# A modulation vector formed by GpSimd beside the delta rule

## The reference

```python
mod = jax.nn.silu(c) @ w_ada[layer] + b_ada[layer]      # (1, 1024) @ (1024, 3072)
shift, scale, gate = jnp.split(mod[:, None, :], 3, axis=-1)
h = rms_norm(x, norm_g[layer]) * (1.0 + scale) + shift
```

## Time and profile before

| | us |
|---|---|
| median of three runs | 3007.29 |
| lowest, highest | 3001.44, 3011.1 |
| the profiled execution | 3002.61 |
| its span | 3000.8 |
| mean granted clock of TensorE | 0.963 of full |
| TensorE busy | 2821.8 |
| VectorE busy | 1661.6 |
| GpSimd busy | 928.9 |
| ACT busy | 676.1 |

### The profile page before, as it was taken

How to read it: one execution, slowest core, us unless ns; L and a number is a source line. 1 busy time by engine, 2 the same in 40 slices (tenths; PEclk the granted TensorE clock), 3 DMA queues, 4 the chain that set the end, 5 groups by cost and what they waited for, 6 DMA issues and landing times.

```text
span 3000.8 us, 34181 instructions
## 1 busy us (share of the span) xinstructions
PE 2821.8 (94%) x14231; PEld 2381.3 (79%) x14231; DVE 1661.6 (55%) x2160; ACT 676.1 (23%) x1063; POOL 928.9 (31%) x510
## 2 busy tenths in 40 slices
PE   6999999989998999999999998999999999978798
PEld 5787799877777788878888877788888888867577
DVE  4789755664512555454444478522465556466556
ACT  3112222233322420000000032211222222234342
POOL 1422000016631613332332235653111221211454
PEclk9999888889999999999999999999999999989899
DMA  3223223225311421111111134552322333354573
GB/s 136 65 92 116 77 82 99 74 68 191 125 56 64 155 92 50 49 57 42 43 56 43 42 108 159 203 169 92 127 92 99 99 118 121 117 191 172 197 263 133
DMA packets 134270, 325.10 MB, mean 108 GB/s; under 512 B 11724, under 2 KB 49508, under 8 KB 133988
## 3 DMA queue, kind: packets, MB, share of 16 engines
q1 hardware_dynamic: 61632, 165.70, 17.3%
q10 hardware_dynamic: 72484, 157.22, 14.6%
HBM read 245.26 MB, written 77.61 MB: 108 GB/s over the span
## 4 chain that ended last, share of the span: by engine, by line
PE 77%; DVE 12%; ACT 3%; DMA 3%; issue 2%; POOL 1%; ACTq 1%; DVEq 0%; POOLq 0%
PE pp L286 25%; PE pp L268 21%; PE pp L471 7%; PE pp L1931 5%; PE pp L2506 4%; DMA ret_m<-m_s 2%; PE pp L1176 2%; PE pp L1406 1%; PE pp L1837 1%; DVE ffn_cb L2111 1%; POOL w_lo L3088 1%; PE pp L1429 1%; DVE hgin_b L2321 1%; PE pp L1817 1%; PE pp L1433 1%
## 5 line engine op out<-in xcount | busy, mean ns | idle before, releaser
L3086 POOL CAST w_hi<-w_raw 128x1024 fp32r<-128x1024 f32 x252 | 292.9, 1162 | 1976.9 <-PE pp L286 844.8
L3088 POOL TENSOR_TENSOR w_lo<-w_raw,w_hi 128x1024 fp32r<-128x1024 f32 x252 | 640.5, 2542 | 20.2
L286 PE MATMUL pp<-w_hi,act_hi 128*128 128x512 f32 x1344 | 548.8, 408 | 25.7 <-POOL w_lo L3088 10.5
L286 PE MATMUL pp<-w_hi,act_lo 128*128 128x512 f32 x1344 | 532.8, 396 | 0.0
L286 PE MATMUL pp<-w_lo,act_hi 128*128 128x512 f32 x1344 | 531.4, 395 | 0.0
L286 PEld LDWEIGHTS pp<-w_hi,act_hi 128*128 128x128 f32 x1344 | 257.6, 192 | 84.8 <-POOL w_lo L3088 15.3
L286 PEld LDWEIGHTS pp<-w_hi,act_lo 128*128 128x128 f32 x1344 | 256.8, 191 | 59.4
L286 PEld LDWEIGHTS pp<-w_lo,act_hi 128*128 128x128 f32 x1344 | 257.7, 192 | 51.6
L268 PE MATMUL pp<-act_lo,w_hi 128*128 128x512 f32 (+1 forms) x944 | 290.7, 389 | 0.0
L268 PE MATMUL pp<-act_hi,w_hi 128*128 128x512 f32 (+1 forms) x944 | 290.7, 389 | 0.0
L268 PE MATMUL pp<-act_hi,w_lo 128*128 128x512 f32 (+1 forms) x944 | 290.6, 389 | 0.0
(11 more groups left out here) (393 smaller groups left out, 4131.7 us busy)
## 6 DMA issues: line engine op xcount, KB each, us to landing
w_raw<-in_weights SPq DMA_DIRECT2D x292, 512.0 KB, 3.5
z_s<-hg_st ACTq DMA_DIRECT2D x52, 512.0 KB, 3.0
hg_qkb<-hT_s SPq DMA_DIRECT2D x18, 512.0 KB, 7.1
qkvT_s<-mixin_o ACTq DMA_DIRECT2D x12, 512.0 KB, 2.8
gdn_qkv<-qkvT_s ACTq DMA_DIRECT2D x8, 768.0 KB, 5.0
front_x<-in_x ACTq DMA_DIRECT2D x8, 512.0 KB, 5.7
mix_x<-in_x ACTq DMA_DIRECT2D x8, 512.0 KB, 5.5
x_s<-mix_y ACTq DMA_DIRECT2D x8, 512.0 KB, 2.9
```

The source lines that it names most:

```text
L286: last = pe.matmul(dst, a[:, k, t * P:(t + 1) * P], columns(w, j, k, 0, n), start=(k == 0 and a is high and w is w_hi), stop=(k == NK - 1 ...
L3086: pool.tensor_copy(hi, raw).then_inc(w_split, 1)
L3088: pool.tensor_tensor(lo, raw, hi.bitcast(F32), ALU.subtract).then_inc(w_ready, 1)
```

## The change

GpSimd gets a new routine, `sum_ada`, which it runs after `move_mem`. For each of the twelve strips and each half it multiplies the half (four k by 256 columns) by `ada_c`, repeated over the columns, in one 128x1024 instruction, counts the half as let go, adds four blocks to two (128x512), and two to one (128x256); for the second half it adds the two halves too. That is seven dependent instructions, each waited for through `ada_summed`. The sums and the products lie in the space of `w_hi`, free in these rounds. TensorE then adds over partitions only: two matmuls a strip, with the sum stationary and a column of ones moving. It waits for the strip's seven steps instead of the loads, and counts `ada_turned`, for which VectorE waits instead of `w_ready`. GpSimd splits the first output weights only when all twelve are kept.

```diff
+            def sum_ada(self, pool):
+                after(pool, self.src.an, f"gate{self.src.GATES - 1}", 0)
+                tt, n = pool.tensor_tensor, 0
+
+                def step(ins):
+                    nonlocal n
+                    n += 1
+                    ins.then_inc(self.ada_summed, 1)
+                    pool.wait_ge(self.ada_summed, n)
+
+                m = self.ada_parts
+                for j, out in enumerate(self.ada_sum):
+                    strip = FIRST_STRIP[f"ada{j}"]
+                    for half in range(2):
+                        pool.wait_ge(w_loaded[half], (RAW_AT[strip] // 2 + 1) * 16)
+                        pool.wait_ge(w_ready, halves_ready(strip, half))
+                        w = w_raw[:, half * HALF:(half + 1) * HALF].rearrange("p (k n) -> p k n", n=SC)
+                        c = ada_c[:, half * NK // 2:(half + 1) * NK // 2].rearrange("p (k a) -> p k a", a=1).broadcast_to((P, NK // 2, SC))
+                        step(tt(m[:, :, :], w, c, ALU.mult))
+                        pool.sem_inc(w_ready, 1)
+                        step(tt(m[:, 0:2, :], m[:, 0:2, :], m[:, 2:4, :], ALU.add))
+                        if half == 0:
+                            step(tt(out[:, :], m[:, 0, :], m[:, 1, :], ALU.add))
+                        else:
+                            step(tt(m[:, 0, :], m[:, 0, :], m[:, 1, :], ALU.add))
+                            step(tt(out[:, :], out[:, :], m[:, 0, :], ALU.add))
+                assert n == self.ADA_STEPS * N_ADA
+
+            ADA_STEPS = 7
...
                 def ada(j):
-                    strip = FIRST_STRIP[f"ada{j}"]
                     if j:
                         pe.wait_ge(self.ada_kept, j)
                     if prep:
                         after(pe, self.pv, "l3", p)
-                    for half in range(2):
-                        pe.wait_ge(w_loaded[half], (RAW_AT[strip] // 2 + 1) * 16)
+                    pe.wait_ge(self.ada_summed, (j + 1) * self.ADA_STEPS)
                     for m in range(2):
-                        for k in range(NK):
-                            c = k * SC + m * P
-                            last = pe.matmul(bank(self.K_)[:, m:m + 1], w_raw[:, c:c + P], ada_c[:, k:k + 1], start=(k == 0), stop=(k == NK - 1))
-                            if m == 1 and k == NK // 2 - 1:
-                                last.then_inc(w_ready, 1)
-                    last.then_inc(w_ready, 1)
+                        last = pe.matmul(bank(self.K_)[:, m:m + 1], self.ada_sum[j][:, m * P:(m + 1) * P], ones[:, 0:1], start=True, stop=True)
+                    last.then_inc(self.ada_turned, 1)
...
                 def ada(j):
-                    dve.wait_ge(w_ready, halves_ready(FIRST_STRIP[f"ada{j}"], 2))
+                    dve.wait_ge(self.ada_turned, j + 1)
...
                     delta.move_mem(pool)
+                    delta.sum_ada(pool)
+                    pool.wait_ge(delta.ada_kept, N_ADA)
                     pool.wait_ge(w_ready, halves_ready(j, 0))
```

More of the change, by code:

```diff
@@ L172, in build @@
         w_raw = place("w_raw", [P, STRIP])
+        w_hi_at = top["at"]
         w_hi = [place(f"w_hi{s}", [P, HALF], F32R) for s in range(4)]
@@ L1050, in __init__ @@
                 self.mem_moved, self.mem_kept = sem("gdn_mem_moved"), sem("gdn_mem_kept")
+                ada_sums = {"at": w_hi_at}
+                self.ada_sum = [place(f"gdn_ada_sum{j}", [P, SC], F32, ada_sums) for j in range(N_ADA)]
+                self.ada_parts = place("gdn_ada_parts", [P, NK // 2, SC], F32, ada_sums)
+                assert ada_sums["at"] <= w_hi_at + 4 * 4 * HALF
+                self.ada_summed = sem("gdn_ada_summed")
                 self.ada_stored, self.ada_turned = sem("gdn_ada_stored"), sem("gdn_ada_turned")
@@ L1363, in act @@
                     if o == NT - 1:
-                        act.wait_ge(self.ada_turned, 1)
+                        act.wait_ge(self.ada_turned, N_ADA + 1)
                         act.activation(self.mr[:, :], bank(self.F_)[0:3 * NK, 0:P], ACT.Copy).then_inc(self.ada_turned, 1)
-                        act.wait_ge(self.ada_turned, 2)
+                        act.wait_ge(self.ada_turned, N_ADA + 2)
                         act.dma_start(mod_s.rearrange("o (c p) -> (o c) p", p=P), self.mr[:, :]).then_inc(self.ada_stored, 16)
```

## The result

The changed kernel takes 3022.7 us in the median of four runs (3019.4 to 3024.2), the kernel before 3006.3 (now four runs): ratio 1.0059, 95% interval 1.0043 to 1.0074. It is slower, by 18 us if one goes by the ratio (16 between the medians); 38 were forecast. The profiled execution's span is 3022.4 us. L1639 and L1642 are now the steps that take a level's result (L1609, L1612); take care not to read the new L1639 as the old mask.

The account below looks back on a forecast made before the run. TensorE was taken to bound the rounds. Rounds 4 to 7 (+17 us), 1 to 3 (+20) and 0 (+2.5), less 1 or 2 for existing waits, gave +38 on 3007.3: 3045 us, range 3020 to 3078.

Parts of the forecast that it names:

- TensorE's work: In the ada product, L1406: 48.7 us of matmuls go, 6 us of one-column products come, 43 us gained if nothing else happened.
- No slack before a first strip: Before a round's first strip: round 1's loads land at 401.6 us and L1406 starts at 401.95, so no slack.
- GpSimd's price: GpSimd's seven steps: multiply 2.34 us, adds 1.2 and 0.65, with pauses 9.6 us a strip, 115 in twelve.
- Rival C: GpSimd's multiply with a repeated input costs 4.7 us, making the kernel dearer: 3074 to 3103 us; chance 0.12.
- First strip: Before L1418 in round 1: the sum comes 4.2 us later with strict turns, 2.7 without; rounds 4 to 7 cost 17 us.
- the turns: In the rounds, GpSimd and some VectorE SBUF steps stop each other for whole instructions; some twenty VectorE steps a round affected.
- Second strips: In rounds 1 to 3, GpSimd's second strip delays VectorE's mask and level 5's result: +7 us a round, +20 in all.
- The sum: Over the eight rounds: 17 + 20 + 2.5 = 39.5 us, less 1 or 2 for existing waits, so +38 us.
- rival A: Only the latency of first strips costs, VectorE's idle time swallowing the turns: +21 us, 3028 us; chance 0.20.
- Rival B: TensorE's clock in the rounds rises over 0.9, since one-column products lower it and waiting does not: 2980 us; chance 0.06.
- three signs of being wrong: In the rounds: VectorE steps keep their times, sums are ready before TensorE asks, or the granted clock rises to 0.95.

Follow-up runs that it names:

- e13: Changed kernel with GpSimd's seven steps replaced by 57 tiny 128x1 memsets a strip, the wait kept: 1.0064 of the kernel before.
- e1: Kernel before, TensorE's 16 products a strip kept, plus GpSimd's seven steps on other data, awaited only by ACT at the rounds' end: 1.0071 of the kernel before.
- e2: Kernel before with only two one-column products a strip, straight from w_raw, and GpSimd idle: 0.9855 of the kernel before.
- e7: e5 with GpSimd's seven steps replaced by tiny memsets, 50 a strip: 2935.5 us, 0.9778 of the kernel before.
- e5: Changed kernel with TensorE's two products a strip moved to the middle of the next round, same GpSimd work: 2991.6 us, 0.9966 of the kernel before.
- e3: Changed kernel with GpSimd's seven steps replaced by long memsets of about the same lengths that read nothing: 1.0023 of the kernel before.
- e14: e1 with chains of tiny 128x1 memsets in place of GpSimd's seven steps: 1.0003 of the kernel before.

## Why the prediction was wrong

The direction, the place and the wait were right; the size was not, 38 us against 18. Its steps in order:

- *TensorE's work.* 48.7 us go and 48 short records come: right (page: 40 us less busy over the program).
- *No slack before a first strip.* Right: the load lands, GpSimd starts 0.1 us later, TensorE stands 5.68 us where it had worked 3.8.
- *GpSimd's price.* 9.6 us a strip forecast, 9.4 measured in round 1 (392.01 to 401.40). The adds were 1.31 and 0.76 for 1.2 and 0.65, the multiply with its repeated input 1.92 for 2.34, with a pause of 0.18 behind it. Rival C, a dear multiply, is out.
- *First strip.* "+4.2 us, against +2.7 without turns." This is the step that failed first. It put the turns on top of the wait, 1.5 us a strip. From the end of t of level 4 to y of level 5, round 1 took 401.95 to 405.72, 3.8 us, before and 395.86 to 402.39, 6.5 us, after: +2.8. The turns I laid end to end with GpSimd's steps hardly stretched those (the multiply of 396.30 took 1.90, and 1.89 is its shortest), and what they cost VectorE fell into TensorE's wait. e13 shows it: no holds, and 6.4 us for the same stretch.
- *Second strips.* "+7 us the round", of which 2.8 for the second strip: the second failed step. I had the next mask end at 417.8, behind a multiply, and VectorE taking level 5's result at 418.2, 9.5 us late. In the trace the mask slipped in at 403.63, in the pause of 0.18 us behind a multiply (and stretched GpSimd's next add from 1.27 to 1.50), and the result was taken at 405.32. From y of level 5 to the next round's L1488 it took 13.0 us before and 12.65 after: nothing. So the two-strip rounds did not come to 52 us (45.4, 42.4, 49.8 and 44.2). The product at the round's end went from 3.6 us to 0.6, which paid for the waits on gdn_mc.
- *The sum.* From the end of t of level 4 to y of level 5 the eight rounds took 34.6 us in all before and 54.9 after: +20.4, where the forecast had 4.2 a round (2.5 for all of round 0). From the end of d of level 6 to the next L1458 or L1488 the four second strips took 16.9 and 14.6: -2.3, where it had three by +2.8. Everything else together moved by +0.7. That is the 18.8 us by which the rounds grew (332.2 to 351.0), and the measured 18. It is rival A's size (+21), though not for A's reason: A said VectorE's idle time swallows the turns, and e1 shows that it doesn't. They are swallowed by TensorE's standing still.
- *Clock.* Rival B was out in the changed kernel (0.84), but half of its mechanism is there. In e2, where only the single columns went, the rounds ran at 0.90. What B had wrong is "waiting does not": the four matmuls of y of level 5 took 1.20 us behind the sixteen products (405.72) and 1.20 behind the wait (402.39), where y of level 4 took 0.61 just before the wait (393.46). With neither the rounds run at 0.95 (e7).

None of the three signs of being wrong came: the VectorE steps were held, the sums came late, the clock stayed. They tested whether the parts exist, and not whether they add.

The error of reasoning was to add two delays that both end at the same instruction. TensorE's y of level 5 waits for the sum and for VectorE; these run side by side, and the later one counts. For each I had priced its cost on the kernel before, where the other is absent.

Not settled: how much of the 53 us between e5 and e7 comes from the waits for VectorE and how much from the clock by itself. The clock was lower behind a wait (above), and no kernel here moves one alone.

## What to carry to other kernels

Work moved to an idle engine can have two prices: its latency in front of whoever needs the result, and the steps of a neighbour that it holds. Where both end at the same instruction, as here, price them there by the maximum and not by the sum, and expect the smaller one to appear when the larger is repaired. A chain of 128x1 memsets in place of the real steps parts the two: it keeps the wait and drops the hold. Match its length to the real wait first; 50, 57 and 67 steps gave three different answers here.

## What the runs showed of the hardware

- There are two kinds of hold. GpSimd's TENSOR_TENSOR held VectorE's steps with two SBUF inputs (L1754 1.53 us in place of 0.42) and its COPY and TENSOR_SCALAR between SBUF tiles (L1647 up to 1.47 us in place of 0.29; L1007, in the kernel before, 2.27 in place of 0.17). A long GpSimd memset held only the latter (e3: L1008 1.64 us, L1646 1.34; L1753 stayed at 0.42). Steps with an input in PSUM were not held by either: L1639 and L1642 of the changed kernel never took over 0.42 us. 672 memsets of one column, 0.10 us each, cost nothing (e14).
- GpSimd's TENSOR_TENSOR with a repeated second input took 1.89 us at the least at 128x1024, where L3088, with two full inputs and an fp32r output, took 2.34; without a repeated input 128x512 took 1.26 and 128x256 0.72.
- In all kernels with the one-column products, the wait or the holds, TensorE's granted clock in the rounds was 0.82 to 0.86. It was 0.90 in e2, with two products a strip and GpSimd idle, and 0.95 in e7, where the same matmuls as in e5 covered 31 us less.
